# The last tile's output projection in two halves by w_out's parts, and the load that its first half releases

## What is computed

```
x = x + jnp.concatenate([o_gla, o_fnet, o_mla], axis=-1) @ w_out[l]
x = x + hier_moe(rms_norm(x, norm2_g[l]), ...)
# hier_moe, for e in 32 experts:
he = jax.nn.silu(t @ w_gate[e]) * (t @ w_up[e])
y = y + combine[:, e:e + 1] * (he @ w_down[e])
```

## Time and profile before

| | us |
|---|---|
| median of 3 runs | 529.92 (528.66 to 530.52) |
| profiled execution | 528.69 |
| its span | 526.9 |
| PE busy | 491.2 (93%) |
| DVE busy | 213.2 (40%) |
| granted clock over the span | 0.985 |

### The profile page before, as it was taken

The page is one execution under the profiler, slowest core; times in us unless marked ns, Lnnn a source line. Parts: engine busy times, 40 slices in busy tenths (PEclk is TensorE's granted clock), DMA queues, the critical chain, the costliest instruction groups (busy, mean ns, idle before and its releaser), DMA issues.

```text
span 526.9 us, 7686 instructions
## 1 busy us (share of the span) xinstructions
PE 491.2 (93%) x2924; PEld 269.3 (51%) x2924; DVE 213.2 (40%) x565; ACT 137.2 (26%) x357; POOL 75.3 (14%) x101
## 2 busy tenths in 40 slices
PE   4999999999999999999999899999999886998893
PEld 3446544557765555455447555555555453454431
DVE  3217320666676671116763423322332212232166
ACT  4404211354476661213131111111111100112023
POOL 1000000361100000001113222222222212111000
PEclk9999999999999999999999999999999989989997
DMA  8996000010199004931089999999999999999974
GB/s 296 359 267 260 2 1 0 16 36 2 33 401 402 4 1 178 416 123 41 2 312 375 418 414 416 413 416 416 418 414 417 414 414 418 418 416 415 403 298 160
DMA packets 40135, 139.95 MB, mean 266 GB/s; under 512 B 9849, under 2 KB 12985, under 8 KB 31905
## 3 DMA queue, kind: packets, MB, share of 16 engines
q1 hardware_dynamic: 34752, 131.38, 63.5%
q0 software_dynamic: 4816, 7.85, 4.0%
q10 hardware_dynamic: 528, 0.22, 0.2%
HBM read 130.47 MB, written 16.39 MB: 279 GB/s over the span
## 4 chain that ended last, share of the span: by engine, by line
PE 64%; DMA 17%; SPq 8%; DVE 7%; issue 2%; ACT 1%; DVEq 0%; ACTq 0%; POOLq 0%
PE bank L747 12%; PE bank L1065 12%; DMA EW<-in_moe_w_up 9%; PE bank L933 9%; PE bank L1078 5%; SPq L615 5%; PE bank L906 5%; PE bank L976 3%; PE bank L965 3%; SPq L620 2%; DMA EW<-y_scratch 2%; DMA EW<-in_w_in 2%; PE bank L1038 2%; PE bank L755 1%; PE bank L853 1%
## 5 line engine op out<-in xcount | busy, mean ns | idle before, releaser
L1065 PE MATMUL bank<-EW,WO 128*64 128x256 f32 x640 | 75.2, 388 | 9.3 <-DMA EW<-in_moe_w_up 7.6
L747 PE MATMUL bank<-EW,XT 128*128 128x512 f32 (+1 forms) x192 | 64.1, 495 | 0.0
L1065 PEld LDWEIGHTS bank<-EW,WO 128*64 128x64 f32 x640 | 45.8, 139 | 33.8 <-DMA EW<-in_moe_w_up 10.2
L933 PE MATMUL bank<-WO,XT 128*128 128x512 f32 x128 | 56.6, 595 | 0.0
L1405 ACT ACTIVATE G<-bank 128x128 f32<-128x128 f32 x32 | 8.9, 278 | 176.6 <-PE bank L1065 172.0
L1769 DVE TENSOR_TENSOR G<-G,bank 128x128 f32<-128x128 f32 x32 | 9.2, 289 | 109.9 <-ACT G L1405 88.9
L1993 POOL DMA_INDIRECT y_scratch<-G,sidx x30 | 30.3, 1010 | 159.9 <-DVE G L1782 148.5
L747 PEld LDWEIGHTS bank<-EW,XT 128*128 128x128 f32 x192 | 32.9, 190 | 31.0 <-issue 31.0
L1782 DVE COPY G<-bank 128x512 f32<-128x512 f32 x32 | 22.1, 692 | 47.6 <-PE bank L1078 47.6
L1078 PE MATMUL bank<-EW,G 128*64 128x512 f32 x160 | 38.3, 599 | 0.0
L933 PEld LDWEIGHTS bank<-WO,XT 128*128 128x128 f32 x128 | 23.7, 190 | 27.3 <-issue 27.3
(11 more groups left out here) (295 smaller groups left out, 633.1 us busy)
## 6 DMA issues: line engine op xcount, KB each, us to landing
EW<-in_moe_w_gate SPq DMA_DIRECT2D x20, 1024.0 KB
EW<-in_moe_w_up SPq DMA_DIRECT2D x20, 1024.0 KB
EW<-in_moe_w_down SPq DMA_DIRECT2D x20, 1024.0 KB
y_scratch<-MIX SPq DMA_DIRECT2D x8, 512.0 KB, 9.2
WO<-in_w_out SPq DMA_DIRECT2D x2, 2048.0 KB, 11.7
MIX<-in_moe_w_gate SPq DMA_DIRECT2D x4, 1024.0 KB
MIX<-in_moe_w_up SPq DMA_DIRECT2D x4, 1024.0 KB
WO<-in_moe_w_gate SPq DMA_DIRECT2D x4, 1024.0 KB
```

The source lines that it names most:

```text
L747: mm = pe.matmul(ps[:, 0:width], xnT[:, c, t * P:(t + 1) * P], w_in_sb[:, c, col:col + width], start=(c == 0), stop=(c == C - 1))
L933: mm = pe.matmul(ps[:, :], xnT[:, c, t * P:(t + 1) * P], w_out_sb[:, c, n * 512:(n + 1) * 512], start=(c == 0), stop=(c == C - 1))
L1065: mm = pe.matmul(bank[BLOCK * m:BLOCK * (m + 1), 0:2 * P].rearrange("p (w n) -> p w n", w=2), xeT[:, c, par * BLOCK:(par + 1) * BLOCK], wv ...
```

## The change

`OUT_ORDER` gets a step "half" for the last tile. ("half", 3, 0) stands where ("out", 3, 0) stood, ("half", 3, 1) where ("out", 3, 1) stood, and ("out", 3, 0), ("out", 3, 1) follow behind it. A half multiplies parts 0 to 3 of w_out, the step "out" of tile 3 only parts 4 to 7. The second half raises a new semaphore `wout_half`; SyncE waits for it instead of all eight projections before it issues gate and up of expert 5. Down of expert 4 is issued after the store of tile 3. The bank plan takes the banks at the halves' places. DVE and ACT have nothing to do at a "half".

```diff
 OUT_ORDER = [...
-             ("L", 1), ("out", 3, 0), ("pos", 1), ("Lf", 2), ("L", 2), ("out", 3, 1), ("pos", 2), ("T", 3), ("pick", 0),
+             ("L", 1), ("half", 3, 0), ("pos", 1), ("Lf", 2), ("L", 2), ("half", 3, 1), ("out", 3, 0), ("out", 3, 1), ("pos", 2), ("T", 3), ("pick", 0),
...
+        elif step[0] == "half":
+            late(("out",) + step[1:])
-        elif step[0] not in ("pick", "norm"):
+        elif step[0] not in ("pick", "norm") and step[0:2] != ("out", T - 1):
             late(step)
...
             for t in range(T):
                 if t == T - 1:
-                    for u in range(T):
-                        for n in range(2):
-                            drained(sp, ("out", u, n))
+                    sp.wait_ge(wout_half, 1)
                     load_gate_up(RING + 1, RING + 1)
-                    load_down(RING, RING)
                 for n in range(2):
                     drained(sp, ("out", t, n))
                 sp.dma_start(x2_d[t * P:(t + 1) * P, :], X[:, t, :]).then_inc(x2_stored, 16)
+            load_down(RING, RING)
...
             for step in OUT_ORDER:
                 kind, t = step[0:2]
-                if kind == "out":
-                    out_part(t, step[2], 4 if t == 0 else 0, C)
+                if kind == "half":
+                    mm = out_part(t, step[2], 0, 4)
+                    if step[2] == 1:
+                        mm.then_inc(wout_half, 1)
+                elif kind == "out":
+                    out_part(t, step[2], 4 if t in (0, T - 1) else 0, C)
```

## The result

The changed kernel is slower. Its median is 535.60 us (534.85 to 536.22, 4 runs), the kernel before 529.29 us (528.09 to 530.52, 4 runs); the ratio is 1.0126, with a 95% interval of 1.0104 to 1.0148. That is 6.3 us more. The forecast was 3.6 us more and a range up to 535.4.

The account below looks back on a forecast made before the run. The experts' weight stream was taken to bound the kernel from about 280 us. PE delay 3.4 + 1.5 = 4.9 us, less slack of 0.6 to 1.4, taken as 3.6 us slower, gave 533.5 us; range 530.6 to 535.4.

Parts of the forecast that it names:

- What bounds the kernel: From about 280 us the experts' weight stream is full; every microsecond of hole in it shows at the end.
- the early load is worth nothing by itself: Ahead of down 6, the 2.10 MB moved early are worth between nothing and the stream's slack, 0.6 to 1.4 us.
- PE's stand: Before pos of tile 1, PE stands about 3.9 us for VectorE's picks; T of tile 3 comes 3.4 to 3.5 us later.
- The clock: After PE stands before pos of tile 1, the granted clock falls; taken as 1.5 us, bounds nothing and 2.8 us.
- one fall: A single drop of PE's clock after the stand before pos of tile 1; 1.5 us, by the row at 446.34.
- two falls: PE's clock dropping twice after the stand; 2.8 us, the upper bound of the clock's price.
- The slack of the stream: From down 6 to expert 9's pair, a later PE is hidden for 0.6 us, tightest at down 5, or 1.4.
- The sum: PE delay 3.4 + 1.5 = 4.9 us at pick_done, less 0.6 to 1.4, is 3.5 to 4.3; 3.6 taken.
- fourth rival: No slack in the weight stream, or the clock falls twice: 4.9 us or more, 534.8 to 536; chance 0.05.

Follow-up runs that it names:

- e1_cover: Changed kernel with out (3, 0)'s parts 4 to 7 back ahead of pos of tile 1, early load of expert 5 kept; 528.93 us, ratio to before 0.9993.
- e2_order_only: Changed kernel's order on PE with SyncE's old waits, so no load is early; 535.96 us, ratio to before 1.0132.
- d4: Kernel before with four dummy matmuls ahead of T of tile 3, nothing else; 532.76 us, ratio 1.0074.
- e3_warm: Changed kernel with four dummy matmuls on PE ahead of pos of tile 1; 532.69 us, ratio to before 1.0077.
- d8: Kernel before with eight dummy matmuls ahead of T of tile 3; 535.21 us, ratio 1.0119.
- e5_half_warm: Changed kernel with two dummy matmuls on PE ahead of pos of tile 1; median 535.50 us, ratio to before 1.0115.
- f2_down5_before: Kernel before with down 5 issued right behind down 6, no early expert 5; 528.41 us, ratio 0.9988.
- f1_down5: e1_cover with down 5 issued right behind down 6; 529.49 us, ratio to before 1.0000.

## Why the prediction was wrong

- **What bounds the kernel, and that the early load is worth nothing by itself:** right, as far as the runs can tell. e1_cover and e2_order_only show it from both sides.
- **PE's stand:** right in place, cause and size: 3.9 us foreseen, 3.76 measured, put down to the last instruction of the picks' chain; 3.4 us of it at T (d4 and e3_warm cost as much: 3.6 and 3.5 us).
- **The clock:** the mechanism right, the size wrong. This is the first of two terms that failed. I took one fall, 1.5 us, by the row at 446.34. Measured: T came 6.4 us later and not 4.9, and taking the low clock away gave back 2.9 us. At 446 us the granted clock was low for some 3.4 us (445.9 to 449.3); here it was low for some 6.8 (255.0 to 261.8), and as long in e2_order_only. At 446 us PE was back at full work at once; here the stand was followed by pos, Lf and L, small pieces with a wait of 0.4 us among them. That these pieces kept the clock low is a guess; no run changes them alone. The bound I gave, 2.8 us for two falls, was right where the value should have been. It also cost the early load most of its lead: issued 1.3 us earlier, not 4.2.
- **The slack of the stream:** the second term, 0.6 to 1.4 us, and 3.6 taken where the sum said 3.5 to 4.3. Measured: none that can be told from zero, in the changed kernel, d4 and d8. The slack was worked out from when each load could have begun with a restart of 1.5 us. That figure came near at down 6 (1.7 us) and failed at down 5, the tightest place, where the restart took about 3 us and the changed kernel moved only 184 and 166 GB/s. That uses up the 0.6 us. Why this restart is slower stays open. And a hole did not give back what the head lost to slow traffic: from 266 to 281 us the changed kernel moved 237 GB/s where 370 went before.
- **The sum with the measured terms:** 3.4 of cover and 3.0 of clock at T of tile 3 (6.4 less 3.4), less nothing, 6.4 us, against 6.3 measured. My fourth rival (no slack, or two falls) gave 4.9 us or more and 534.8 to 536; both of its conditions came together. It had a chance of 0.05, since I held them for separate mishaps. The upper end of the range, 535.4, was 0.2 us short for the same reason.
- **What the pages would have said:** the first-byte latency of 0.6 us of the Trainium skill (DMA: Bandwidth & Descriptors, section Specifications) would have made the slack larger and the forecast worse. It is another quantity than my 1.5 us: in the trace of the kernel before, the first bytes after the issue at 263.92 move in the window from 264.8 to 264.9, 0.9 us after the issue started and 0.6 after it ended, and the stream is at its full rate only after a second gap, from about 265.8 on. The advice of the Trainium skill to issue early and wait late (DMA: Bandwidth & Descriptors, section Rules for kernel authors) gained nothing that these runs can tell; the loads behind the early one were tied to PE. On the clock, the Trainium skill (TensorE: Matmul & The Clock Gate, section What's actually happening) says that "the default state is throttled, and activity releases the throttle"; the trace agrees, 1.00 with dummy work in the stand, 0.62 and 0.53 without.

## What to carry to other kernels

Before splitting a block of matmuls to free a buffer earlier, look at what stands behind it on PE: if that waits for another engine, the block is cover, and what is taken from it is lost again behind it, here 3.4 us for eight instructions. Price a stand of PE with the clock too, and take the whole scatter of the falls and not one row; a few dummy matmuls in the stand are cheap proof. Before issuing a DMA earlier, look at what the loads behind it wait for.

## What the runs showed that I had not expected

A stand of 2.0 us with half the filler left four of five executions at 535 to 536 us and one at 532.6; the same program had two prices, 3 us apart. The length of the stand alone doesn't tell: where PE waits for weights late in the trace of the kernel before, stands of 1.85, 2.10 and 2.70 us were each followed by a fall (a group of 5.36, 5.36 and 5.10 us instead of 3.67) and stands of 1.70 and 1.72 us were not, while in the changed kernel one of 2.28 us was not and in e5_half_warm one of 2.58 us was not. The prediction took the cheapest of the three falls, 1.4 us; the others cost 1.7. And in e1_cover, e2_order_only, e5_half_warm and f2_down5_before the first group of expert 0 ran slow (5.20 to 5.36 us) behind a wait of no more than 0.54 us.

A stream of weight loads that ran empty came back at 39 to 219 GB/s over two to four microseconds, where f1_down5, whose stream was not empty there, moved 415 and 289.
